# Two transformer layers behind a block of gathered experts: layers written out instead of looped, first norm applied after the projection, last down products in two halves

## The chip, the core and the metric

The kernel runs on one core of a Trainium2 chip. The metric is the time of one execution in microseconds (us) on the device; the runs of the kernel before have a median of 1599.08 us.

## What is computed

The reference is a transformer block with product-key experts, then two layers of a second kind, all for 256 rows of width 1024. What matters here is the end of the first block and the layers:

```python
# end of the first block
x = x + g2x * peer(hx2, ...)            # sum over 8 heads x 16 gathered experts for each row
x = rmsnorm(x, final_norm_g)            # final norm of the first block
# second block, two layers
for l in range(2):
    h = rmsnorm_2(x, norm1[l])
    p = h @ w_in[l]                     # columns: q 512, k 128, v 128, u 512
    q = rope(rmsnorm_2(q, q_norm[l])); k = rope(rmsnorm_2(k, k_norm[l]))
    y_f = fourier_mix(u, ...);  y_a = windowed_gqa(q, k, v, sink[l])
    x = x + concat(rmsnorm_2(y_f), rmsnorm_2(y_a)) @ w_o[l]
    h = rmsnorm_2(x, norm2[l])
    up = dwconv_centred(h @ w_up[l], ...)
    x = x + (silu(gate) * val) @ w_down[l]
return x
```

A norm is a scale per row (1 over the root of the row's mean square) and a gain per column. The scale of a row can be applied to the rows of a product instead of to its input.

## The kernel before

The 256 rows are two chunks of 128 partitions, `xr[:, c, :]`. A product in the layers is split in high and low parts: ScalarE rounds a piece of 128x1024 weights to fp32r (`weight_high`, L537), VectorE makes the difference (`weight_rest`, L552), and TensorE computes high x high, high x low and low x high (L1055 to L1057; L1219 to L1221 for the up product). A layer's pieces are 10 for the in-projection (0 to 3 q, 4 and 5 k and v, 6 to 9 u), 8 for the out-projection from `P_O` on, 44 for up from `P_UP`, 22 for down from `P_DOWN`. Three buffers for high and three for low parts go round. The weights come in slots of 2 MB through a ring of four slots, loaded by SyncE's queue in a fixed order; a slot is loaded when the low parts of the slot four before it are done.

The rows of a norm go through TensorE as eight tiles of 128 columns: the old program multiplies the rows with a diagonal that holds the scales (`split_tiles`, L1047), ScalarE takes out the high part with the gain (`tiles_high`, L559), VectorE the rest (`tiles_rest`, L565). So the tiles wait for the row statistics: squares of chunk 0 on ScalarE (L1248), of chunk 1 on VectorE (L1750), variance (L1544, L1545), a root on ScalarE (L1253) and four small steps (`newton`, L1550 to L1553).

Ahead of the layers, the last of 16 stages of gathered experts runs on chunk 1: VectorE makes a dot product of each of 16 gathered rows (L1822), groups of them get their weights (gelu on ScalarE L1389, `wts` on VectorE L1813), ScalarE makes a diagonal of each weight (L1393), and TensorE adds the expert's row (L984). `LAST_ENDS` says after which expert of the last stage weights are handed over. Then VectorE adds the sums to `xr` (`gated`, L1758 and L1759) and applies the block's final norm (L1864).

The order on each engine is that of the code; semaphores tie the engines. The layers are a loop `Fori(0, LAYERS)` on every engine, with the values that waits compare to computed in registers.

## Time and profile before

| what | value |
|---|---|
| runs | 1604.11, 1599.08, 1597.44 us, median 1599.08 |
| profiled execution | 1601.58 us, its span 1599.7 us |
| TensorE busy | 1381.5 us, 86% of the span |
| VectorE busy | 1085.2 us, 68% |
| ScalarE busy | 608.1 us, 38% |
| mean granted TensorE clock | 0.932 of full speed |

The span is the time from the first to the last instruction of the core. PE is TensorE's matmuls, PEld its weight loads, DVE VectorE, ACT ScalarE, POOL GpSimd, SP SyncE. The two layers lie from about 946 us to the end; the last stage of experts ends at 946 us, layer 0 ends at 1271 us, layer 1 at 1593 us.

### The profile page before, as it was taken

To read this page: it belongs to the slowest core of one execution; us is meant where nothing else is said; L and a number is where in the kernel's file an instruction comes from. 1 tells how busy PE (TensorE), PEld (TensorE's weight loads), DVE (VectorE), ACT (ScalarE), POOL (GpSimd) and SP (SyncE) were. 2 spreads that over 40 slices of the span, in tenths; PEclk is the share of its full clock that TensorE was granted. 3 is DMA by queue.
4 is the path that set the end of the run, shared out by engine and by line. 5 is a ranking of instruction groups with operands and counts; after the bars stand their busy time and mean duration, and the time that the engine had idled before them with its cause. 6 is when DMAs were issued, how large, how long until landed. Compare 5 with 4: busy or idle time off the path is not lost.

```text
span 1599.7 us, 19900 instructions
## 1 busy us (share of the span) xinstructions
PE 1381.5 (86%) x6272; PEld 960.2 (60%) x6272; DVE 1085.2 (68%) x2236; ACT 608.1 (38%) x1225; POOL 275.2 (17%) x263
## 2 busy tenths in 40 slices
PE   7998879778797979797987959979999799899998
PEld 2875675434343434343433427669998676699986
DVE  5598745666767676767677566657886466578863
ACT  5244641122222222222222124455665344456652
POOL 0000000633434444444444400000000000000000
PEclk9999979989898989898988989999999999999999
DMA  9425320999999999999999983144454431434440
GB/s 399 200 106 210 139 94 27 400 421 421 422 422 422 422 422 421 422 423 421 422 421 422 421 331 132 53 159 155 162 200 149 180 132 53 159 135 183 179 165 27
DMA packets 49266, 418.02 MB, mean 261 GB/s; under 512 B 5408, under 2 KB 5536, under 8 KB 6560
## 3 DMA queue, kind: packets, MB, share of 16 engines
q0 software_dynamic: 36864, 268.45, 40.4%
q1 hardware_dynamic: 12320, 148.51, 24.2%
q8 instruction: 47, 0.77, 0.2%
q14 instruction: 35, 0.29, 0.0%
HBM read 415.89 MB, written 1.05 MB: 261 GB/s over the span
## 4 chain that ended last, share of the span: by engine, by line
PE 50%; DMA 18%; DVE 12%; issue 10%; POOL 5%; ACT 3%; DVEq 0%; POOLq 0%; ACTq 0%; SPq 0%
DMA arena<-in_uv,ids 16%; PE ps L984 5%; PE ps L1219 5%; PE ps L1220 5%; PE ps L1221 5%; PE ps L1055 4%; PE ps L1057 4%; PE ps L1056 4%; POOL arena L718 3%; POOL ring L718 2%; PE ps L1105 2%; DMA ring<-in_b1w 2%; PE ps L1047 2%; PE ps L837 1%; DVE ring L1822 1%
## 5 line engine op out<-in xcount | busy, mean ns | idle before, releaser
L984 PE MATMUL ps<-ring,arena 128*128 128x512 f32 x512 | 256.5, 664 | 104.3 <-ACT arena L1393 104.3
L984 PEld LDWEIGHTS ps<-ring,arena 128*128 128x128 f32 x512 | 107.8, 214 | 248.4 <-issue 131.9
L1822 DVE CUSTOM_DVE_ANT_0 arena<-arena 128x1024 f32<-128x1024 f32 x128 | 157.0, 1227 | 132.4 <-DMA arena<-in_uv,ids 132.4
L718 POOL DMA_INDIRECT ring<-in_uv,ids x128 | 143.5, 1121 | 546.1 <-issue 306.6
L984 PE MATMUL ps<-arena 128*128 128x512 f32 x512 | 224.5, 596 | 6.8 <-ACT arena L1393 6.8
L552 DVE TENSOR_TENSOR arena_r<-ring,arena_r 128x1024 fp32r<-128x1024 f32 x152 | 185.2, 1224 | 66.3 <-ACT arena_r L537 66.3
L1219 PE MATMUL ps<-hH,arena_r 128*128 128x256 f32 x704 | 199.4, 283 | 0.0
L1220 PE MATMUL ps<-arena_r 128*128 128x256 f32 x704 | 199.2, 283 | 0.0
L1221 PE MATMUL ps<-hH,arena_r 128*128 128x256 f32 x704 | 199.2, 283 | 0.0
L537 ACT ACTIVATE arena_r<-ring 128x1024 fp32r<-128x1024 f32 x152 | 159.1, 1053 | 67.2 <-PE ps L1057 67.2
L984 PEld LDWEIGHTS ps<-arena 128*128 128x128 f32 x512 | 97.5, 191 | 131.6 <-issue 117.8
L1822 DVE CUSTOM_DVE_ANT_0 ring<-ring,arena 128x1024 f32<-128x1024 f32 x128 | 151.0, 1222 | 16.0 <-DMA ring<-in_uv,ids 15.5
L1393 ACT ACTIVATE arena<-cst,wts 128x128 f32<-128x128 f32 x256 | 90.4, 395 | 177.2 <-DVE wts L1813 90.0
L718 POOL DMA_INDIRECT arena<-in_uv,ids x128 | 131.1, 1024 | 86.9 <-PE ps L984 65.4
L1220 PEld LDWEIGHTS ps<-arena_r 128*128 128x128 f32 x704 | 135.2, 192 | 0.0
L1221 PEld LDWEIGHTS ps<-hH,arena_r 128*128 128x128 f32 x704 | 135.2, 192 | 0.0
L1219 PEld LDWEIGHTS ps<-hH,arena_r 128*128 128x128 f32 x704 | 135.2, 192 | 0.0
L1057 PE MATMUL ps<-arena_r 128*128 128x512 f32 (+1 forms) x336 | 127.4, 379 | 0.0
L1055 PE MATMUL ps<-arena_r 128*128 128x512 f32 x240 | 94.3, 393 | 2.6 <-DVE arena_r L583 2.1
L1056 PE MATMUL ps<-arena_r 128*128 128x512 f32 x240 | 93.4, 389 | 0.0
L1389 ACT ACTIVATE gel<-dots 128x4 f32<-128x4 f32 (+1 forms) x66 | 13.5, 205 | 195.5 <-DVE dots L1822 195.4
L1521 ACT ACTIVATE arena<-ps,lp 128x256 f32<-128x256 f32 x88 | 49.8, 566 | 96.5 <-DVE arena L1996 54.1
(272 smaller groups left out, 2105.2 us busy)
## 6 DMA issues: line engine op xcount, KB each, us to landing
ring<-in_lw SPq DMA_DIRECT2D x42, 2048.0 KB, 8.5
ring<-in_b1w SPq DMA_DIRECT2D x18, 2048.0 KB, 9.0
wqb<-in_wq SPq DMA_DIRECT2D x8, 1024.0 KB
ring<-in_lw SPq DMA_DIRECT2D x6, 1024.0 KB, 5.1
ring<-in_uv,ids POOLq DMA_INDIRECT x128, 22.3
arena<-in_uv,ids POOLq DMA_INDIRECT x128, 23.3
cst<-in_const SPq DMA_DIRECT2D x1, 1736.0 KB, 21.3
skb<-in_ctx SPq DMA_DIRECT2D x1, 1024.0 KB, 14.1
```

Of the source, the lines that this page charges most:

```text
L537: nc.scalar.activation(wH[p % PIECES], piece_raw(p), ACT.Copy).then_inc(w_hi, 1)
L552: nc.vector.tensor_tensor(wL[p % PIECES], piece_raw(p), wH[p % PIECES].bitcast(F32), ALU.subtract)\
L718: pool.indirect_dma_start(pairs_at[k], None, uv, bass.IndirectOffsetOnAxis(ap=ids[:, c, k:k + 1], axis=0))\
L984: last = nc.tensor.matmul(ps[:, 4 + 2 * c + b, :], diag[:, k % 4, :], vrows[k][:, b * 512:(b + 1) * 512], start=False, stop=(close and k = ...
L1055: nc.tensor.matmul(dst, ah, wH[p % PIECES][:, cols_], start=first, stop=False, skip_group_check=True)
L1056: nc.tensor.matmul(dst, ah, wL[p % PIECES][:, cols_], start=False, stop=False, skip_group_check=True)
L1057: last = nc.tensor.matmul(dst, al, wH[p % PIECES][:, cols_], start=False, stop=end, skip_group_check=True)
L1219: nc.tensor.matmul(dst, high, hH[:, k, :], start=(k == 0), stop=False)
L1220: nc.tensor.matmul(dst, high, hL[:, k, :], start=False, stop=False)
L1221: last = nc.tensor.matmul(dst, wL[p % PIECES][:, k * P:(k + 1) * P], hH[:, k, :], start=False, stop=(k == KD - 1))
L1393: nc.scalar.activation(diag[:, k % 4, :], ident, ACT.Copy, scale=wts[:, c, k:k + 1])\
L1822: V.tensor_tensor_reduce(out=urows[k], in0=urows[k], in1=hrow[:, c, :], scale=1.0, scalar=0.0, op0=ALU.mult, op1=ALU.add, accum_out=dots[: ...
```

## The change

It has five parts. The layers are written out (no loop; `lpv` reads the layer's parameters in place, so the copy `lp` goes). The first norm of a layer is no longer applied ahead of the projection: TensorE transposes the raw rows (`raw_tiles`, four tiles when the left half of `xr` is ready, four when the right half is), and the row scales `rs1` are applied when ScalarE takes the projection out. In layer 0 the final norm of the first block is taken out in the same way: its gain goes into the layer's gain (`fgc`), its scale `pre` into `rs1`. The high and low parts of pieces 0 and 1 get buffers of their own and are made ahead of the layer's opening. The last three down pieces compute their left halves first, then their right halves; `xr` is added up in halves, and the output is stored in four parts. The last stage of experts hands over at other places (`LAST_ENDS`).

```diff
-LAST_ENDS = (4, 8, 12, 14, 15, 16)
+LAST_ENDS = (4, 8, 10, 12, 13, 14, 15, 16)
...
+        first_wH = [area(kb, PIECE, of=arena_r) for kb in (0, 22)]
+        first_wL = [area(kb, PIECE, of=arena_r) for kb in (4, 8)]
...
+        def high_of(l, p):
+            return first_wH[p] if p < 2 else wH[(l * (PL - 2) + p - 2) % PIECES]
+
+        def low_of(l, p):
+            return first_wL[p] if p < 2 else wL[(l * (PL - 2) + p - 2) % PIECES]
+
+        def buffers_free(act, l, p):
+
+            if p >= 2 + PIECES:
+                act.wait_ge(piece_used, l * PL + p - PIECES + 1)
+            elif l == 0 and p < 2:
+                act.wait_ge(pair_free, NS + TOPK * (STAGES - 1) + 12)
+            elif l == 0:
+                act.wait_ge(l_half, 2)
+            elif p < 2:
+                act.wait_ge(piece_used, (l - 1) * PL + P_DOWN + 12)
+            else:
+                act.wait_ge(piece_used, l * PL + p - 2 - PIECES + 1)
...
-            with sp.Fori(0, LAYERS - 1) as l:
+            for l in range(LAYERS):
...
-            sp.wait_ge(l_x, LAYERS + 1)
-            sp.dma_start(out.rearrange("(c p) d -> p c d", p=P), xr[:, :, :]).then_inc(out_done, 16)
-            sp.wait_ge(out_done, 16)
+            for i in range(4):
+                c, part = i % 2, slice((i // 2) * 512, (i // 2 + 1) * 512)
+                sp.wait_ge(dn_out, 4 * LAYERS - 3 + i)
+                sp.dma_start(out[c * P:(c + 1) * P, part], xr[:, c, part]).then_inc(out_done, 16)
+            sp.wait_ge(out_done, 64)
...
+                def raw_tiles(*tiles):
+
+                    for k in tiles:
+                        if k >= 6:
+                            pe.wait_ge(lo_out, l * S_TILES + S_NORM1 + k - 5)
+                        for c in range(NC):
+                            last = nc.tensor.transpose(stile(S_NORM1, k)[:, c * P:(c + 1) * P], xr[:, c, k * P:(k + 1) * P],
+                                                       ident)
+                        last.then_inc(stile_done, 1)
...
-                pe.wait_ge(l_rows, 2 * l + 1)
-                split_tiles(S_NORM1, xr)
-
-                rows_by(0, 512, (4, 5), hH, hL, S_NORM1)
+                pe.wait_ge(l_half, 2 * l + 1)
+                raw_tiles(0, 1, 2, 3)
+                rows_by(0, 512, (4, 5), hH, hL, S_NORM1, (0,))
+                pe.wait_ge(l_half, 2 * l + 2)
+                raw_tiles(4, 5, 6, 7)
+                rows_by(0, 512, (4, 5), hH, hL, S_NORM1, (1, 2, 3))
...
+                for k in range(FT - PIECES):
+                    down(k, range(2))
+                for k in range(FT - PIECES, FT):
+                    last = down(k, (0,), False)
+                last.then_inc(dn_half, 1)
+                for k in range(FT - PIECES, FT):
+                    down(k, (1,))
...
-            table(ACT.Sqrt)
+            weight_high(act, 0, 0)
             act.wait_ge(wo_out, 6)
             squares(xr, ss, 0, 1, waste=junk_h)
             act.sem_inc(sq_done, 1)
-            roots(2, 5)
-
-            with act.Fori(0, LAYERS) as l:
+            weight_high(act, 0, 1)
+
+            act.wait_ge(l_par, 1)
+            for l in range(LAYERS):
                 off = l * (L_TILES // 2)
-                chain.enter(l, 9)
-                table(ACT.Sqrt)
-                act.wait_ge(l_x, l + 1)
-                squares(xr, ss, 0, 1)
-                act.sem_inc(sq_done, 1)
-                roots(2, l * 4 + 6)
-                weight_high(act, l, 0)
-                act.wait_ge(l_par, l + 1)
-                tiles_high(act, l, S_NORM1, hH, lpv("n1"))
-                weight_high(act, l, 1, 2, 3, 4)
+                tiles_high(act, l, S_NORM1, hH, lpv(l, "n1"))
+                weight_high(act, l, 2)
+                if l == 0:
+                    table(ACT.Sqrt)
+                    roots(2, 5)
+                    weight_high(act, l, 3)
+                    act.wait_ge(l_x, 1)
+                    squares(xr, ss, 0, 1)
+                    act.sem_inc(sq_done, 1)
+                    weight_high(act, l, 4)
+                    roots(2, l * 4 + 6)
+                else:
+                    squares(xr, ss, 0, 1)
+                    act.sem_inc(sq_done, 1)
+                    weight_high(act, l, 3)
+                    roots(2, l * 4 + 6)
+                    weight_high(act, l, 4)
+                act.wait_ge(l_scale, l + 1)
...
+                            nc.scalar.activation(qraw2[:, c, :], src, ACT.Copy, scale=rs1[:, c:c + 1]).then_inc(lproj_out, 1)
...
+                if l + 1 < LAYERS:
+                    weight_high(act, l + 1, 0, 1)
+                    table(ACT.Sqrt)
...
-            for c in range(NC):
-                dve.wait_ge(pair_free, NS + TOPK * (STAGES - 1 + c))
-                gated(g2b, [(c, n, 4 + 2 * c + n) for n in range(2)], 4 + 2 * c)
-            square_of_chunk1()
-            dve.wait_ge(sq_done, 5)
-            variance(2, D)
-            newton(2, 5)
-            for c in range(NC):
-                run(V.scalar_tensor_tensor(xr[:, c, :], xr[:, c, :], rstd[:, c:c + 1], con("fg"), ALU.mult, ALU.mult))
-            dve.wait_ge(lpar_in, 16)
+            dve.wait_ge(pair_free, NS + TOPK * (STAGES - 1))
+            gated(g2b, [(0, n, 4 + n) for n in range(2)], 4)
+            weight_rest(dve, 0, 0, 1)
+            dve.wait_ge(pair_free, NS + TOPK * STAGES)
+            for n in range(2):
+                gated(g2b, [(1, n, 6 + n)], 6 + n)
+                dve.sem_inc(l_half, 1)
...
+                def statistics(call, *between):
+
                     square_of_chunk1()
-                    if call == 6:
-                        V.tensor_copy(lp[:, :], lps[:, bass.ds(l, 1), :].rearrange("p a n -> p (a n)")).then_inc(l_par, 1)
-                    dve.wait_ge(sq_done, l * 4 + call)
+                    dve.wait_ge(sq_done, call)
                     variance(2, D)
-                    newton(2, l * 4 + call)
+                    weight_rest(dve, l, *between)
+                    newton(2, call)
+
+                tiles_rest(dve, l, S_NORM1, hL, hH, lpv(l, "n1"))
+                weight_rest(dve, l, 2)
+                if l == 0:
+                    statistics(5, 3)
+                    run(V.tensor_copy(pre, rstd[:, 0:2]))
+                    dve.wait_ge(stile_done, S_NORM1 + KD)
                     for c in range(NC):
-                        last = V.tensor_scalar(scale_diag[:, c, :], ident, rstd[:, c:c + 1], None, ALU.mult)
-                    last.then_inc(l_rows, 1)
-
-                normed(6)
-                dve.wait_ge(l_par, l + 1)
-                weight_rest(dve, l, 0)
-                tiles_rest(dve, l, S_NORM1, hL, hH, lpv("n1"))
-                weight_rest(dve, l, *range(1, P_O - 2))
+                        run(V.scalar_tensor_tensor(xr[:, c, :], xr[:, c, :], pre[:, c:c + 1], con("fg"), ALU.mult, ALU.mult))
+                    dve.sem_inc(l_x, 1)
+                    statistics(6, 4)
+                    run(V.tensor_tensor(rs1, rstd[:, 0:2], pre, ALU.mult))
+                else:
+                    statistics(l * 4 + 6, 3)
+                    run(V.tensor_copy(rs1, rstd[:, 0:2]))
+                    weight_rest(dve, l, 4)
+                dve.sem_inc(l_scale, 1)
+                weight_rest(dve, l, *range(5, P_O - 2))
...
-                dve.wait_ge(piece_used, (l + 1) * PL)
-                for i in range(4):
-                    dst = xr[:, i % 2, (i // 2) * 512:(i // 2 + 1) * 512]
-                    V.tensor_tensor(dst, dst, ps[:, 4 + i, :], ALU.add).then_inc(dn_out, 1)
-                dve.wait_ge(dn_out, 4 * l + 4)
-                dve.sem_inc(l_x, 1)
-                chain.leave(LAYERS)
+                if l + 1 < LAYERS:
+                    weight_rest(dve, l + 1, 0, 1)
+                for n in range(2):
+                    if n == 0:
+                        dve.wait_ge(dn_half, l + 1)
+                    else:
+                        dve.wait_ge(piece_used, (l + 1) * PL)
+                    for c in range(NC):
+                        dst = xr[:, c, n * 512:(n + 1) * 512]
+                        V.tensor_tensor(dst, dst, ps[:, 4 + 2 * n + c, :], ALU.add).then_inc(dn_out, 1)
+                    dve.wait_ge(dn_out, 4 * l + 2 * n + 2)
+                    dve.sem_inc(l_half, 1)
```

On TensorE nothing is added or taken in the products; the 16 matmuls of a first norm's tiles become 16 transposes. On VectorE 301 register instructions of the loop's body go.

The order of VectorE's instructions between the experts and layer 0. Before (`xr` the rows, `sm` small vectors, `arena` scratch; L1759 is the last addition of chunk 1, L1864 the final norm, the branch the loop's entry):

```order
L1759 TENSOR_TENSOR xr<-xr,arena 128x512
L1750 ISA arena,sm<-xr 128x1024
L1750 ISA sm 128x1
L1544 TENSOR_SCALAR sm<-sm 128x2
L1545 RECIPROCAL sm<-sm 128x2
L1550 TENSOR_TENSOR sm<-sm 128x2
L1551 TENSOR_TENSOR sm<-sm 128x2
L1552 TENSOR_SCALAR sm<-sm 128x2
L1553 TENSOR_TENSOR sm<-sm 128x2
L1864 SCALAR_TENSOR_TENSOR xr<-xr,sm,cst 128x1024 x2
L1871 UNCONDITIONAL_BRANCH
```

The same engine and place after the change (L573 is a low part of weights, L1811 and L1812 an addition of half a chunk, L589 the rests of the tiles):

```order
L1812 TENSOR_TENSOR xr<-xr,arena 128x512
L573 TENSOR_TENSOR arena_r<-ring,arena_r 128x1024 x2
L1811 TENSOR_TENSOR arena<-ps,wqb 128x512
L1812 TENSOR_TENSOR xr<-xr,arena 128x512
L1811 TENSOR_TENSOR arena<-ps,wqb 128x512
L1812 TENSOR_TENSOR xr<-xr,arena 128x512
L589 SCALAR_TENSOR_TENSOR arena_r<-ps,lps,hH 128x256 x8
L573 TENSOR_TENSOR arena_r<-ring,arena_r 128x1024
L1803 ISA arena,sm<-xr 128x1024
L1803 ISA sm 128x1
```

Two low parts of weights now stand between the additions of chunk 0 and those of chunk 1, and the statistics have moved behind the tiles' rests.

ScalarE at the same place, before (L1243 loads a table, L1248 squares of chunk 0, L537 a high part of weights, L559 high parts of tiles; L127, L1252 and L370 are waits):

```order
L1243 ACT_TABLE_LOAD
L1243 ACTIVATE sm<-cst 128x1
L127 ISA
L1428 REGISTER_ALU
L1248 ACTIVATE arena,sm<-xr 128x1024
L127 REGISTER_ALU
L1252 ISA
L1253 ACTIVATE sm<-sm 128x2
L370 ISA
L537 ACTIVATE arena_r<-ring 128x1024
```

And after, from the last diagonal on (L558 is the high part, L1289 the squares, L583 the tiles' high parts, L1294 the root, L1493 the eviction of q):

```order
L558 ACTIVATE arena_r<-ring 128x1024
L1289 ACTIVATE arena,sm<-xr 128x1024
L558 ACTIVATE arena_r<-ring 128x1024
L583 ACTIVATE hH<-ps,lps 128x256 x8
L558 ACTIVATE arena_r<-ring 128x1024
L1284 ACT_TABLE_LOAD
L1284 ACTIVATE sm<-cst 128x1
L1294 ACTIVATE sm<-sm 128x2
L558 ACTIVATE arena_r<-ring 128x1024
L1289 ACTIVATE arena,sm<-xr 128x1024
L558 ACTIVATE arena_r<-ring 128x1024
L1294 ACTIVATE sm<-sm 128x2
```

The first high part now stands ahead of the squares of chunk 0, and each further one between two steps of the statistics.

## Rows read from the trace of the kernel before

**Rows 1.** Windows: stretch, its us, PE, PEld, DVE, ACT, POOL busy, granted clock, DMA, GB/s

```profile
1084.00:1210.00 126.00, 126.00 (x1053) 126.00 (x1052) 105.71 (x170) 78.52 (x128) 0.00 (x0) 1.00 0.48 177
...
1210.00:1271.00 61.00, 60.81 (x272) 50.17 (x271) 28.82 (x30) 24.91 (x29) 0.00 (x0) 1.00 0.49 182
...
958.50:965.00 6.50, 6.46 (x33) 6.46 (x34) 3.97 (x7) 3.19 (x7) 0.00 (x0) 0.56 0.01 3
```

**Rows 2.** Timeline, last stage of experts: start, us, instruction, idle before it

```profile
920.63 7.13 PE L984 MATMUL ps<-ring,arena 128*128 128x512 f32 x16 [2.70 <-ACT arena L1393]
...
930.57 15.43 PE L984 MATMUL ps<-arena 128*128 128x512 f32 x32 [2.81 <-ACT arena L1393]
...
928.72 1.23 DVE L1822 CUSTOM_DVE_ANT_0 arena<-arena 128x1024 f32<-128x1024 f32 x1 [1.25 <-DMA arena<-in_uv,ids]
...
931.20 1.22 DVE L1822 CUSTOM_DVE_ANT_0 arena<-arena 128x1024 f32<-128x1024 f32 x1 [1.12 <-DMA arena<-in_uv,ids]
...
938.05 0.22 DVE L1813 SCALAR_TENSOR_TENSOR wts<-prob,pz,gel 128x1 f32<-128x1 f32 x1 [0.56 <-ACT gel L1389]
...
946.11 0.69 DVE L1758 TENSOR_TENSOR arena<-ps,wqb 128x512 f32<-128x512 f32 x1 [3.79 <-PE ps L984]
```

**Rows 3.** Timeline of TensorE: scaled tiles of layer 0, and piece 5

```profile
958.54 6.52 PE L1047 MATMUL ps<-arena,xr 128*128 128x128 f32 x32 [12.54 <-DVE arena L1883]
...
979.67 0.39 PE L1055 MATMUL ps<-arena_r,hH 128*128 128x256 f32 x1 [0.51 <-DVE arena_r L552]
```

**Rows 4.** SyncE, the first three weight loads of layer 0, and their times to landing

```profile
936.12 1.29 SPq L667 DMA_DIRECT2D ring<-in_lw  x3
...
DMA to landing us min/median/max: 8.1/10.2/14.6
```

**Rows 5.** Timeline, the steps of layer 0's opening on ScalarE and VectorE

```profile
942.41 1.06 ACT L1248 ACTIVATE arena<-xr 128x1024 f32<-128x1024 f32 x1 [1.26 <-DVE xr L1759]
...
964.57 1.52 DVE L565 SCALAR_TENSOR_TENSOR arena_r<-ps,lp,hH 128x256 fp32r<-128x256 f32 x3 [0.37 <-ACT hH L559]
...
976.33 1.09 ACT L1443 ACTIVATE arena<-ps 128x512 f32<-128x512 f32 x2 [4.38 <-PE ps L1057]
...
977.30 2.96 ACT L537 ACTIVATE arena_r<-ring 128x1024 fp32r<-128x1024 f32 x3
...
978.39 3.50 DVE L552 TENSOR_TENSOR arena_r<-ring,arena_r 128x1024 fp32r<-128x1024 f32 x3 [5.18 <-ACT arena_r L537]
```

**Rows 6.** Timeline of TensorE, four transposes in the scores of layer 0

```profile
1041.49 0.60 PE L1148 MATMUL ps<-cst,arena 128*128 128x128 f32 x4
```

**Rows 7.** Timeline of VectorE, small steps in straight code and in the loop

```profile
951.51 0.16 DVE L1553 TENSOR_TENSOR sm<-sm 128x2 f32<-128x2 f32 x1
...
951.71 2.61 DVE L1864 SCALAR_TENSOR_TENSOR xr<-xr,sm,cst 128x1024 f32<-128x1024 f32 x2
...
957.80 0.16 DVE L1553 TENSOR_TENSOR sm<-sm 128x2 f32<-128x2 f32 x1
...
958.00 0.48 DVE L1883 TENSOR_SCALAR arena<-cst,sm 128x128 f32<-128x128 f32 x2
```

**Rows 8.** Timeline between the layers, VectorE and ScalarE

```profile
1270.85 2.48 DVE L2027 TENSOR_TENSOR xr<-xr,ps 128x512 f32<-128x512 f32 x4 [5.84 <-PE ps L1057]
...
1276.54 1.22 DVE L1750 CUSTOM_DVE_ANT_0 arena<-xr 128x1024 f32<-128x1024 f32 x1 [3.21 <-issue]
...
1267.94 1.28 ACT L1243 ACT_TABLE_LOAD   x1 [4.19 <-issue]
...
1299.78 3.50 DVE L552 TENSOR_TENSOR arena_r<-ring,arena_r 128x1024 fp32r<-128x1024 f32 x3 [5.18 <-ACT arena_r L537]
```

**Rows 9.** Timeline of VectorE's last instructions, and DMA issues: size, us to landing

```profile
1592.85 2.48 DVE L2027 TENSOR_TENSOR xr<-xr,ps 128x512 f32<-128x512 f32 x4 [5.84 <-PE ps L1057]
...
out_x<-xr SPq DMA_DIRECT2D x1, 1024.0 KB, 3.9
...
cst<-in_const SPq DMA_DIRECT2D x1, 105.5 KB, 2.0
```

132 lines of the change are left out of this document (65 added, 67 removed).

## The prediction

> **What bounds the kernel now.** I read the stages by windows first, then the timeline of each place where one stage hands over to the next. Inside the two layers TensorE is the bound for most of the time: it is busy for the whole 126.0 us of the 44 up pieces and for 60.8 us of the 61 us of the 22 down pieces [rows 1]. That makes 126/44 = 2.86 us for a piece of 24 products of 256 columns and 60.8/22 = 2.76 us for a piece of 12 products of 512 columns. The change leaves the number of these products alone, so nothing is won there. What it touches are three hand-overs: from the last experts to layer 0, from layer 0 to layer 1, and from layer 1 to the output. I work out for each when "piece 5" of the in-projection starts, the last piece before the heads' norm chain, because everything behind it (squares, rotation, scores) is the same before and after and simply shifts with it.
>
> **The hand-over from the experts (before).** TensorE does experts 4 to 7 in 7.13 us, then waits, and does 8 to 15 from 930.57 in 15.43 us, to 946.0 [rows 2]. VectorE waits 3.79 us for that end and starts adding chunk 1 at 946.11. Then come square, statistics and final scaling of both chunks, a second square and second statistics, the diagonal, and only at 958.54 does TensorE start again, with scaled tiles that take 6.52 us [rows 2, 3]. Piece 5 starts at 979.67 [rows 3].
>
> **Single last experts.** After the change the last stage hands weights over after experts 4, 8, 10, 12, 13, 14, 15, 16. The dot products come every 2.48 us: the group that starts TensorE at 930.57 covers four of them, and with two the weights are ready two products, about 5 us, earlier, which is before TensorE has finished experts 4 to 7 at 927.8. From there it is fed: a single expert takes 7.13/4 = 1.8 us, 8 to 11 end at 934.9, and 12, 13, 14 follow close on their weights. The last weight is at 938.05 [rows 2], its diagonal some 0.7 us later, and the last expert ends at about 941.5, some 4.5 us earlier. Added are two more small weights on VectorE and two on ScalarE, at 0.22 us each, in time in which both wait for gathers.
>
> **Low parts first takes this gain back.** In the new order VectorE adds chunk 0, then makes the low parts of pieces 0 and 1, and only then adds chunk 1. These low parts wait for ScalarE's high parts, and these for the first 2 MB of layer weights. Its load is issued at 936.12, when the last gather has landed, and lands 8.1 us later, at 944.2 (the smallest of the three in the row) [rows 4]. From there: high part 0 (1.0 us each, 2.96 for three [rows 5]) to 945.3; low part 0 (3.50 for three, 1.23 with its latency) to 946.5; meanwhile ScalarE squares chunk 0 (1.06 and some 0.2 more) to 946.5, high part 1 to 947.55, low part 1 to 948.8. Chunk 1 is added from 948.8 on, **2.7 us later than before**, although the experts ended 4.5 us sooner. Queued behind that wait are all of chunk 1's additions, and behind them TensorE's tiles. The four operations take 2.9 us: the left half is done at 950.3, the right one at 951.7.
>
> **Raw tiles, scales later.** Now TensorE starts at 950.3 with transposes of unscaled rows. Four transposes of 128x128 take 0.60 us [rows 6] where the 16 scaled products took 6.52. But TensorE has stood since 941.5, and the clock will be at its lower level, 1.2 GHz, as it was in the stretch of the scaled tiles, where the row shows 0.56 [rows 1]. Those tiles used to take the slow time on themselves; now piece 0 does. Four tiles: 950.3 to 952. VectorE's rests, 0.51 us each (three in 1.52) [rows 5], start at 951.7, so tiles 0 and 1 are ready at 952.75. Piece 0 takes 2.76 us at the full clock and 5.4 at half; I take 4.0, since the clock came back some way into the scaled tiles: end at 956.7. The other four tiles follow: 956.7 to 957.9. ScalarE has their high parts at 958.95 (0.5 each, like VectorE's), then high part 2 to 960.0, VectorE low part 2 to 961.3, piece 2 on TensorE to 964.05. Then statistics stand between the low parts. Square of chunk 1 1.2 us and two small steps to 962.9, root 963.1, high part 3 to 964.2, low part 3 to 965.4, the four small steps 0.8, a copy 0.2, final scaling of both chunks 2.61 [rows 7]: 969.0. Second square 1.3 and variance to 971.0; ScalarE squares chunk 0 from 969.1, high part 4 to 971.4, low part 4 to 972.65, four small steps and a product: the projection's scale is ready at 973.65. ScalarE takes out q (two in 1.09) to 974.75, makes high part 5, VectorE low part 5, and **piece 5 starts at 977.1**. Before, the same tail after piece 3 is seen in [rows 5]: 976.33, 977.30, 978.39. Gain: 979.67 - 977.1 = **2.6 us**. With the full clock in piece 0 it is 3.8, with half the clock throughout 1.4.
>
> **Between the layers.** Call T the moment when the last down product ends: 1270.8. Before: adding 2.48 us, then VectorE stands 3.21 and ScalarE 4.19 with nothing that they wait for, at the loop's jump back; then square, the copy of the layer's parameters, statistics, diagonal, scaled tiles. Piece 5's low part starts at 1299.78 [rows 8], so piece 5 at about 1301.0 (1.28 behind it, as in layer 0: 978.39 and 979.67): **T + 30.2**. After: the last three pieces do their left halves first. The third one needs its low part 2.7 us after the fourth-last piece ends, and it is there at 2.4 (the splitting of a piece is ScalarE 1.06, VectorE 1.23 behind the freed buffer), so nothing stalls. The right halves take 3 x 1.38 = 4.1 us, in which VectorE makes the two low parts of layer 1 and adds the left half. At T TensorE turns four tiles at once; VectorE adds the right half (half of 2.48) to T + 1.3, makes two rests to T + 2.3. Piece 0 to 5.1, four tiles to 6.2, piece 1 to 8.9. High parts of tiles to 7.35, high part 2 to 8.4, low part 2 to 9.65, square 10.9, variance 11.3, low part 3 12.5, four steps and copy 13.5, low part 4 14.7. TensorE: piece 2 to 12.4, piece 3 to 15.3. From there the known tail of 3.35: evictions 1.09, high part 5, low part 5. **Piece 5 at T + 18.6.** Gain **11.6 us**. This is the large term, and it needs the clock to stay up: TensorE's holes are about 1.3 us here, where it used to stand for the whole hand-over.
>
> **The end.** Before, from the last product at 1592.8: 2.48 us of adding, one store of 1 MB that lands in 3.9 us, span end at 1599.7, so 6.9 us [rows 9]. After: the left half is added and on its way before the last product ends; behind it come 1.3 us of adding and two stores of 256 KB, the second issued at + 1.4. A store's time lies between 2.0 (the 105.5 KB load) and 3.9; I take 2.4, nearer to the small one: + 3.8, and 0.4 to the span's end. Gain **2.7 us**, between 1.2 and 3.1.
>
> **The layers written out.** The register instructions that computed wait values in the loop are gone, 301 of them on VectorE. Do they cost something? A chain of small steps advances 0.20 us a step in straight code (951.51 to 951.71) and 0.20 in the loop (957.80 to 958.00) [rows 7]. I take 0. The jump back is counted above. The Trainium skill (Runtime: NRT & Kernel Launch, "Instruction fetch mechanics") says that a taken branch outside the window stalls for its code while straight code is prefetched; the 3.21 and 4.19 us at the jump are in line with it. By that rule the written-out layers have no such stall, as in my sum.
>
> **Sum.** 2.6 + 11.6 + 2.7 = 16.9 us. The profiled execution's own time is 1601.58 (span 1599.7): it becomes 1584.7. The median of the runs is 1599.08, 2.5 lower, and what the comparison will go by: **1582.2 us**.
>
> **Rivals.**
> (a) The clock takes part of it back. The openings have holes of 1 to 2 us on TensorE, and between experts 7 and 8 a hole of 2.8 us was enough for the slow start that makes eight experts 15.43 instead of 14.26 [rows 2]. If piece 0 is slow throughout in layer 0 (+1.2) and pieces 0 and 1 of layer 1 are slow too (tiles 4 to 7 2.6 us later, piece 3 to 19.5, piece 5 at T + 22.8: +4.2), the gain is 11.5 and the time 1587.6. The Trainium skill (TensorE: Matmul & The Clock Gate, "Part 4: PE-mode transpose") states that transposes do not count as busy for the clock as matmuls do. By it the raw tiles, unlike the scaled ones, wake nothing, and this rival is what would happen; no stretch of this trace has transposes behind a low clock, so it is not tested here.
> (b) More than I count: the register instructions do cost where two engines answer each other (the scores of eight head groups, about 40 answers a layer). At 0.1 us an answer it is 8 us for both layers: 1574. The equal steps in [rows 7] speak against it.
> (c) No change within the measurement: the chain behind piece 5 is held by something else that doesn't shift. Against it: in the code nothing but ScalarE's evictions and squares stands between piece 5 and VectorE's norm of the heads. Its time: only 2.7 at the end and a few at the jump, 1592 to 1597.
> (d) Slower. Written out, the layers' code is twice as long, and all of it comes in by DMA beside the weights. If TensorE, which eats it fastest, ran dry, each time at the 3 to 4 us that the jump cost, it would take five such stalls to eat the 16.9 and eight to be slower by over 0.5%. Against it: the first pass through the loop is straight code too, and the 126 us stretch has no hole [rows 1].
>
> **Chances.** The sum as worked out, 0.70 (own range 1577 to 1586); (a) 0.14; (b) 0.08; (c) 0.05; (d) 0.03. A measurement of this kernel can tell about 0.5% from no change, 8 us: faster means under 1591.1. Faster takes the sum, (a) and (b) and a little of (c): 0.94; same 0.04; slower 0.02. The range for 8 in 10 takes (a) in and half of (b): **1575 to 1588**. The terms' own bounds make it no wider: +1.2/-1.2 at the first hand-over, +1.5/-0.4 at the end, and some 3 us between runs.
>
> **What the profile after would show.** Right: the last experts end near 941.5, and VectorE's additions of chunk 1 start near 948.8 behind a wait for ScalarE's high part 1; TensorE idle about 9 us there; piece 5 near 977; after the last down product of layer 0 piece 5 about 18.6 us later, with no VectorE idle time put down to issue; about 4.2 us from the last product to the end; up and down stretches at 126.8 and 60 us as before. Wrong: the granted clock at half in layer 1's opening, or TensorE holes between pieces 1 to 4 longer than 1 us, would say that the statistics between the low parts are too dear; more than 20 us gained would say that the loop's instructions cost something in the layer's body.

## The result, and the profile after

The changed kernel takes 1584.29 us (median of four runs, 1583.28 to 1588.16), against 1599.34 for four runs of the kernel before: a ratio of 0.9912, 95% interval 0.9894 to 0.9930, or 15.05 us less. That is more than the half per cent that can be told from no change, and 2.1 us above the 1582.2 that were forecast. Its profiled execution took 1588.16 us (span 1586.4), the slowest of the four, so the spans differ by 13.3 us only.

| what | before | after |
|---|---|---|
| span of the profiled execution | 1599.7 | 1586.4 |
| TensorE busy | 1381.5 (86%) | 1377.8 (87%) |
| VectorE busy | 1085.2 (68%) | 1082.2 (68%) |
| ScalarE busy | 608.1 (38%) | 606.1 (38%) |
| granted TensorE clock, mean | 0.932 | 0.938 |

**The last experts and the start of layer 0.** The timeline after; each row is start, us, instruction, and in brackets the idle time before it and what ended it. TensorE, VectorE and ScalarE in turn (L1005 experts, L1066 raw tiles, L1084 the first product of a group, L1875 dot product, L1811 and L1812 additions, L573 and L558 low and high parts of weights, L589 and L583 those of the tiles, L1803 square of chunk 1, L1952 the heads' norm). They answer to [rows 2, 3, 5].

```profile
928.45 14.11 PE L1005 MATMUL ps<-arena 128*128 128x512 f32 x32
950.92 1.94 PE L1066 MATMUL ps<-cst,xr 128*128 128x128 f32 x8 [8.37 <-DVEq L1917]
953.78 0.80 PE L1084 MATMUL ps<-arena_r,hH 128*128 128x512 f32 x1 [0.92 <-DVE arena_r L589]
...
958.28 1.03 PE L1066 MATMUL ps<-cst,xr 128*128 128x128 f32 x8
...
973.81 0.39 PE L1084 MATMUL ps<-arena_r,hH 128*128 128x256 f32 x1 [4.14 <-DVE arena_r L573]
...
978.27 0.34 PE L1084 MATMUL ps<-arena_r,hH 128*128 128x256 f32 x1
```

```profile
937.00 1.23 DVE L1875 CUSTOM_DVE_ANT_0 arena<-arena 128x1024 f32<-128x1024 f32 x1 [1.09 <-DMA arena<-in_uv,ids]
...
946.02 1.23 DVE L573 TENSOR_TENSOR arena_r<-ring,arena_r 128x1024 fp32r<-128x1024 f32 x1 [2.85 <-ACT arena_r L558]
948.17 1.23 DVE L573 TENSOR_TENSOR arena_r<-ring,arena_r 128x1024 fp32r<-128x1024 f32 x1 [0.92 <-ACT arena_r L558]
949.31 0.68 DVE L1811 TENSOR_TENSOR arena<-ps,wqb 128x512 f32<-128x512 f32 x1
...
951.60 0.69 DVE L1812 TENSOR_TENSOR xr<-xr,arena 128x512 f32<-128x512 f32 x1
...
959.20 1.66 DVE L589 SCALAR_TENSOR_TENSOR arena_r<-ps,lps,hH 128x256 fp32r<-128x256 f32 x4 [4.69 <-ACT hH L583]
...
962.39 1.22 DVE L1803 CUSTOM_DVE_ANT_0 arena<-xr 128x1024 f32<-128x1024 f32 x1
...
976.94 2.36 DVE L573 TENSOR_TENSOR arena_r<-ring,arena_r 128x1024 fp32r<-128x1024 f32 x2 [2.33 <-ACT arena_r L558]
...
983.98 1.22 DVE L1952 TENSOR_REDUCE sm<-arena 128x16 f32<-128x1024 f32 x1 [3.19 <-ACT arena L1503]
```

```profile
944.87 1.06 ACT L558 ACTIVATE arena_r<-ring 128x1024 fp32r<-128x1024 f32 x1 [5.29 <-DMA ring<-in_lw]
...
958.70 1.57 ACT L583 ACTIVATE hH<-ps,lps 128x256 fp32r<-128x256 f32 x4 [5.32 <-PE ps L1066]
```

The experts end at 942.56 (forecast 941.5; before 946.0), 4.3 us earlier after the last gathered row than before. The 32 matmuls start 3.0 us earlier, at 928.45, since the first group behind experts 4 to 7 is smaller, and they run 1.3 us shorter, without the slow start of [rows 2]. VectorE then stands 2.85 and 0.92 us behind ScalarE's high parts, and ScalarE 5.29 us behind the first weights. So chunk 1 is added only from 949.31 (forecast 948.8; before 946.11), and TensorE stands 8.37 us. All three waits stand where the prediction put them. The weights were issued at 936.99 here and at 936.12 before [rows 4]; the last gather landed 0.87 us later in this execution. I take that for chance: over the fourteen profiled executions of this document it landed anywhere from 933.7 to 938.9, with no order by kernel. Piece 5 starts at 978.27: 1.4 us earlier than before, 2.3 us with that 0.87 taken out. The forecast was 2.6. TensorE also stands 4.14 us ahead of piece 4, whose low part is queued behind the statistics, and piece 4 then takes 4.46 us (973.81 to 978.27) where it took 2.9 before.

**Between the layers**, VectorE and TensorE after, which answer to [rows 8] (L2095 additions, two operations to a row):

```profile
1268.01 1.28 DVE L2095 TENSOR_TENSOR xr<-xr,ps 128x512 f32<-128x512 f32 x2
1271.74 1.28 DVE L2095 TENSOR_TENSOR xr<-xr,ps 128x512 f32<-128x512 f32 x2 [2.46 <-PE ps L1086]
...
1289.41 3.49 DVE L573 TENSOR_TENSOR arena_r<-ring,arena_r 128x1024 fp32r<-128x1024 f32 x3 [3.44 <-ACT arena_r L558]
1296.44 1.22 DVE L1952 TENSOR_REDUCE sm<-arena 128x16 f32<-128x1024 f32 x1 [3.54 <-ACT arena L1503]
```

```profile
1271.54 1.03 PE L1066 MATMUL ps<-cst,xr 128*128 128x128 f32 x8
1274.11 0.50 PE L1084 MATMUL ps<-arena_r,hH 128*128 128x512 f32 x1 [1.53 <-DVE arena_r L589]
...
1276.98 1.04 PE L1066 MATMUL ps<-cst,xr 128*128 128x128 f32 x8
...
1281.32 0.47 PE L1084 MATMUL ps<-arena_r,hH 128*128 128x512 f32 x1 [0.57 <-DVE arena_r L573]
...
1290.69 0.39 PE L1084 MATMUL ps<-arena_r,hH 128*128 128x256 f32 x1 [0.76 <-DVE arena_r L573]
```

The last product ends at T = 1271.7. No idle time is put down to issue any more. The steps come at T + 2.4, 5.3, 9.6 and, for piece 5, 19.0; forecast were 2.3, 5.1, 9.65 and 18.6. Before it was T + 30.2.

**The end**, VectorE, which answer to [rows 9], and the page's line on the stores:

```profile
1582.62 1.28 DVE L2095 TENSOR_TENSOR xr<-xr,ps 128x512 f32<-128x512 f32 x2 [2.80 <-PE ps L1086]
```

```profile
out_x<-xr SPq DMA_DIRECT2D x4, 256.0 KB, 2.0
```

From the last product to the end of the span it is 3.8 us (forecast 4.2, before 6.9), with 2.0 us for a store of 256 KB where 2.4 were taken.

**The granted clock**, windows: stretch, its us, PE, PEld, DVE, ACT and POOL busy, granted clock, DMA share, GB/s. They answer to [rows 1].

```profile
947.00:957.50 10.50, 5.66 (x17) 4.52 (x18) 5.81 (x10) 2.75 (x5) 0.00 (x0) 0.51 0.84 357
974.00:978.00 4.00, 4.00 (x22) 4.00 (x22) 1.56 (x5) 3.15 (x4) 0.00 (x0) 0.57 0.00 0
1035.50:1043.00 7.50, 6.53 (x8) 2.71 (x9) 1.05 (x5) 0.29 (x3) 0.00 (x0) 0.54 0.00 0
1085.00:1211.00 126.00, 126.00 (x1053) 126.00 (x1052) 105.88 (x171) 78.34 (x128) 0.00 (x0) 1.00 0.48 177
...
1262.00:1290.00 28.00, 25.84 (x131) 21.19 (x129) 16.82 (x29) 14.62 (x23) 0.00 (x0) 1.00 0.47 180
```

The up stretch is what it was: busy throughout, at full clock. Between the layers the clock stays at 1.00 through raw tiles and holes. At the experts' end it goes to its lower level, 1.2 GHz, after TensorE has stood from 942.56 to 947.0, and stays there over the raw tiles and the larger part of piece 0. It falls a second time at 974.4, behind the 4.14 us that TensorE stands and 0.6 us into piece 4, and stays low over that piece until 977.8. This stretch is new too: before, the clock was at 1.00 there. The row at 1035.5 is new as well: before, that place of layer 0 ran at full clock. It is TensorE's products of 512 columns for the Fourier mix, first before, then after:

```profile
1037.54 3.67 PE L1036 MATMUL ps<-ring,arena 128*128 128x512 f32 x8 [1.97 <-DVE arena L1922]
```

```profile
1036.47 6.75 PE L1057 MATMUL ps<-ring,arena 128*128 128x512 f32 x8 [1.81 <-DVE arena L1981]
```

Eight matmuls take 6.75 us instead of 3.67.

### The profile page after: what moved, and what is told of

Same layout as the page of the kernel before. It is cut to its first block, busy times and chain, and to the rows that moved or that the text cites. A ratio compares the mean times of both kernels' runs of the same rounds, so it can differ in the third digit from the quotient of the medians.

```text
span 1586.4 us, 18714 instructions
## 1 busy us (share of the span) xinstructions
PE 1377.8 (87%) x6240; PEld 952.9 (60%) x6240; DVE 1082.2 (68%) x2236; ACT 606.1 (38%) x1225; POOL 272.8 (17%) x263
## 3 DMA queue, kind: packets, MB, share of 16 engines
q1 hardware_dynamic: 12624, 148.52, 24.7%
## 4 chain that ended last, share of the span: by engine, by line
PE 49%; DMA 17%; DVE 14%; issue 9%; POOL 6%; ACT 4%; POOLq 0%; DVEq 0%; ACTq 0%; SPq 0%
DMA arena<-in_uv,ids 15%; PE ps L1252 5%; PE ps L1254 5%; PE ps L1253 5%; PE ps L1005 5%; PE ps L1084 4%; PE ps L1085 4%; PE ps L1086 4%; POOL arena L739 3%; POOL ring L739 2%; PE ps L1138 2%; DVE ring L1875 2%; DMA ring<-in_b1w 2%; PE ps L858 2%; PE ps L859 1%
## 5 line engine op out<-in xcount | busy, mean ns | idle before, releaser
L1005 PE MATMUL ps<-ring,arena 128*128 128x512 f32 x512 | 255.8, 663 | 106.0 <-ACT arena L1434 106.0
L1005 PEld LDWEIGHTS ps<-ring,arena 128*128 128x128 f32 x512 | 107.5, 213 | 250.0 <-issue 131.5
L1875 DVE CUSTOM_DVE_ANT_0 arena<-arena 128x1024 f32<-128x1024 f32 x128 | 156.9, 1226 | 134.6 <-DMA arena<-in_uv,ids 124.6
L573 DVE TENSOR_TENSOR arena_r<-ring,arena_r 128x1024 fp32r<-128x1024 f32 x152 | 185.2, 1223 | 63.9 <-ACT arena_r L558 63.9
L1005 PE MATMUL ps<-arena 128*128 128x512 f32 x512 | 224.2, 594 | 3.7 <-ACT arena L1434 3.7
L1252 PE MATMUL ps<-hH,arena_r 128*128 128x256 f32 x704 | 199.4, 283 | 0.0
L558 ACT ACTIVATE arena_r<-ring 128x1024 fp32r<-128x1024 f32 x152 | 159.1, 1053 | 68.7 <-PE ps L1086 63.0
L1005 PEld LDWEIGHTS ps<-arena 128*128 128x128 f32 x512 | 96.5, 190 | 129.2 <-issue 116.2
L1875 DVE CUSTOM_DVE_ANT_0 ring<-ring,arena 128x1024 f32<-128x1024 f32 x128 | 151.0, 1221 | 16.0 <-DMA ring<-in_uv,ids 15.5
L1252 PEld LDWEIGHTS ps<-hH,arena_r 128*128 128x128 f32 x704 | 135.1, 192 | 0.0
L1084 PE MATMUL ps<-arena_r 128*128 128x512 f32 x240 | 94.4, 393 | 1.9 <-DVE arena_r L607 1.6
L1430 ACT ACTIVATE gel<-dots 128x4 f32<-128x4 f32 (+2 forms) x68 | 13.9, 204 | 205.4 <-DVE dots L1875 205.3
L1572 ACT ACTIVATE arena<-ps,lps 128x256 f32<-128x256 f32 x88 | 49.6, 564 | 96.8 <-DVE arena L2058 57.3
```

Source lines behind the costliest of these rows:

```text
L558: nc.scalar.activation(high_of(l, p), piece_raw(p), ACT.Copy).then_inc(w_hi, 1)
L573: nc.vector.tensor_tensor(low_of(l, p), piece_raw(p), high_of(l, p).bitcast(F32), ALU.subtract)\
L1005: last = nc.tensor.matmul(ps[:, 4 + 2 * c + b, :], diag[:, k % 4, :], vrows[k][:, b * 512:(b + 1) * 512], start=False, stop=(close and k = ...
L1084: nc.tensor.matmul(dst, ah, high_of(l, p)[:, cols_], start=first, stop=False, skip_group_check=True)
L1252: nc.tensor.matmul(dst, high, hH[:, k, :], start=(k == 0), stop=False)
L1875: V.tensor_tensor_reduce(out=urows[k], in0=urows[k], in1=hrow[:, c, :], scale=1.0, scalar=0.0, op0=ALU.mult, op1=ALU.add, accum_out=dots[: ...
```

## The experiments

Twelve kernels were run, each in four to twelve executions beside the kernel before on the same chip. The median of before was 1600.27 beside the first four, 1599.76 beside the next four, 1601.41 beside the three after them and 1599.44 beside the last; so the ratios are compared, or the medians within a group. For each profiled execution I take the distances between five marks. g is the start of the last gathered row's dot product; the layer's first weights are issued in the same moment, so differences in the gathers fall out. c1 is the end of chunk 1's additions, sq the start of its square on VectorE, hn the start of the heads' norm (the first operation that is the same in all), T the start of VectorE's additions behind the last down product. The row of after is worked out from the rows above (937.00, 951.60 + 0.69, 962.39, 983.98, 1271.74, 1296.44); the others from the same places of their traces. The distances of a row are those of one execution. Where a low stretch of the clock lies over TensorE's work, a distance grows by 0.8 to 3 us without any edit: the scaled tiles of layer 0, the same code, take 6.76 us in e1 and 5.31 in e2.

| kernel | median us | ratio to before (95%) | g to c1 | g to sq | g to hn | hn to T | T to hn, layer 1 | hn to T, layer 1 | T to end |
|---|---|---|---|---|---|---|---|---|---|
| before | 1599.34 | | 12.9 | 12.9 | 48.9 | 285.8 | 35.6 | 286.4 | 6.9 |
| changed | 1584.29 | 0.9912 (0.9894 to 0.9930) | 15.3 | 25.4 | 47.0 | 287.8 | 24.7 | 286.2 | 3.8 |
| e1 | 1594.66 | 0.9970 (0.9958 to 0.9982) | 13.1 | 13.2 | 49.4 | 284.0 | 31.8 | 285.7 | 6.9 |
| e2 | 1591.68 | 0.9944 (0.9927 to 0.9960) | 13.1 | 13.2 | 47.9 | 285.8 | 31.2 | 286.0 | 3.8 |
| e3 | 1585.09 | 0.9904 (0.9888 to 0.9921) | 15.1 | 25.8 | 48.3 | 285.7 | 24.7 | 285.8 | 3.7 |
| e4 | 1582.04 | 0.9884 (0.9866 to 0.9902) | 9.2 | 22.9 | 45.2 | 285.6 | 24.7 | 285.8 | 3.8 |
| e5 | 1585.47 | 0.9907 (0.9891 to 0.9924) | 13.1 | 25.8 | 47.9 | 285.5 | 24.7 | 285.8 | 3.8 |
| e6 | 1585.94 | 0.9909 (0.9888 to 0.9930) | 15.3 | 26.4 | 48.8 | 285.7 | 24.7 | 285.8 | 3.8 |
| e6t | 1584.58 | 0.9909 (0.9890 to 0.9928) | 15.5 | 25.4 | 47.8 | 285.7 | 24.7 | 285.8 | 3.8 |
| e7 | 1572.11 | 0.9838 (0.9818 to 0.9857) | 9.2 | 15.9 | 37.5 | 285.4 | 23.1 | 284.0 | 3.8 |
| e9 | 1572.13 | 0.9820 (0.9805 to 0.9835) | 9.2 | 16.6 | 38.2 | 285.4 | 23.1 | 284.0 | 3.8 |
| e10 | 1580.84 | 0.9883 (0.9863 to 0.9903) | 9.2 | 20.0 | 41.6 | 287.7 | 24.7 | 286.2 | 3.8 |
| e8 | 1571.60 | 0.9820 (0.9802 to 0.9838) | 9.2 | 15.9 | 37.5 | 285.7 | 23.1 | 284.1 | 3.8 |
| e11 | 1577.36 | 0.9868 (0.9845 to 0.9890) | 15.2 | 20.1 | 41.8 | 285.6 | 23.1 | 284.1 | 3.7 |

**e1, written out only.** The kernel before with the layers written out and nothing else.

```diff
-            with dve.Fori(0, LAYERS) as l:
+            for l in range(LAYERS):
```

> The kernel before with its two layers written out and nothing else. My sum: only the stall at the jump back goes, 3.1 us (VectorE's 3.21 us of idle time put down to issue between the layers); the steps inside the layers keep their 0.20 us, so the time is 1596. Rival (the register instructions cost something wherever engines answer each other): 8 us or more, 1591 or less. Rival (code comes in too slowly): slower than before.

Measured 1594.66, 4.8 us less by the ratio (2.9 to 6.7). The opening of layer 1, start of the rows on VectorE:

```profile
1267.39 2.48 DVE L2024 TENSOR_TENSOR xr<-xr,ps 128x512 f32<-128x512 f32 x4 [5.84 <-PE ps L1057]
1270.07 1.22 DVE L1748 CUSTOM_DVE_ANT_0 arena<-xr 128x1024 f32<-128x1024 f32 x1 [0.20 <-DVE xr L2024]
```

Between the additions and the square there are now 0.20 us where before there were 3.21 put down to issue. T to hn is 3.8 us shorter. The other distances also shrink: hn to T by 1.8 in layer 0 and 0.7 in layer 1. Of these, 0.6 to 0.7 us in each layer lies between hn and the second norm (91.85 to 91.18, 93.49 to 92.87), where the scores' small steps are and the wait values were computed. The other 1.1 us in layer 0 are the clock's. They lie in the scaled tiles of the second norm, first before, then e1:

```profile
1077.44 6.79 PE L1047 MATMUL ps<-arena,xr 128*128 128x128 f32 x32 [5.82 <-DVE arena L1883]
```

```profile
1075.12 5.58 PE L1047 MATMUL ps<-arena,xr 128*128 128x128 f32 x32 [5.72 <-DVE arena L1880]
```

Before, the granted clock fell at 1076.8, late in TensorE's idle time, and stayed low until 1083.7, over nearly all the tiles; in e1 it fell at 1072.0 and was back at 1078.8.

**e2, written out and halves.** Adds the last three down pieces in halves and the store in four parts.

```diff
+                for k in range(FT - PIECES, FT):
+                    last = down(k, (0,), False)
+                last.then_inc(dn_half, 1)
+                for k in range(FT - PIECES, FT):
+                    down(k, (1,))
```

> The same with the last three down pieces in halves, the left half added while the right one is computed, and the output stored in four parts; the norm still ahead of the projection. My sum: 2.7 to 3.1 us at the end (6.85 us from the last product to the span's end become 3.8), and 1.25 us between the layers (half of the 2.48 us of adding), so 4.2 us on top of the written-out kernel: 1592. What is left to the changed kernel's 1584.3, some 7.5 us, is then the price of the norm ahead of the projection. Rival: the halves are hidden or cost as much as they bring, same as written out only.

Measured 1591.68, 3 us below e1. The end is 3.1 us shorter, as in the changed kernel; between the layers only 0.6 us are won by it, not the 1.25 of half the additions.

**e3, old ends.** The changed kernel with the experts in the old groups.

```diff
-LAST_ENDS = (4, 8, 10, 12, 13, 14, 15, 16)
+LAST_ENDS = (4, 8, 12, 14, 15, 16)
```

> The changed kernel with the old places at which the last experts' weights are handed over (4, 8, 12, 14, 15, 16). My theory: the last expert ends 4.5 us later, near 947, but VectorE gets to chunk 1 only at 949.3, behind the low parts, so the single experts bring nothing: within 0.3 us of the changed kernel, 1584.3. Rival: they carry their full 4.5 us, then this is 1588.8.

Measured 1585.09, ratio 0.9904 against 0.9912. Its experts, and the start of chunk 1's additions on VectorE (g is 938.68):

```profile
933.12 15.70 PE L1005 MATMUL ps<-arena 128*128 128x512 f32 x32 [2.81 <-ACT arena L1434]
```

```profile
950.75 0.68 DVE L1811 TENSOR_TENSOR arena<-ps,wqb 128x512 f32<-128x512 f32 x1
```

The experts end 10.1 us after g instead of 5.6, yet chunk 1's additions start at g + 12.1, as with the new ends (+ 12.3). The single experts bring nothing in this order, as the prediction had it. That hn comes 1.3 us later after g than in the changed kernel is mostly the clock: piece 0 takes 5.3 us for 4.5 and piece 4 0.8 us more.

**e4, chunk 1 first.** The changed kernel with chunk 1's additions ahead of the two low parts on VectorE.

```diff
-            weight_rest(dve, 0, 0, 1)
             dve.wait_ge(pair_free, NS + TOPK * STAGES)
             for n in range(2):
                 gated(g2b, [(1, n, 6 + n)], 6 + n)
                 dve.sem_inc(l_half, 1)
+            weight_rest(dve, 0, 0, 1)
```

> The changed kernel, but VectorE adds chunk 1 (and releases the halves of xr) before the low parts of pieces 0 and 1. My theory: the low parts in front hold chunk 1 from 942.5 to 949.3. Without them the additions are done at 945.5, TensorE's tiles are there early, low part 1 ends at about 949.3 as now and two rests later, near 950.4, piece 0 starts (953.8 now): 3.4 us of gain at most, less what ScalarE's order (high parts and squares ahead of the tiles) takes: 1581.5. Rival: the low parts in front are right, and this only moves the same work: 1584.3.

Measured 1582.04, 3 us below e3 on the same chip; their intervals overlap, so the marks have to carry it (g to hn 45.2 against 48.3). Chunk 1 is done at g + 9.2 and TensorE has raw tiles early, but the first piece starts only 3.5 us earlier, since both parts of weight 1 now stand ahead of the tiles' parts. TensorE:

```profile
946.00 1.12 PE L1066 MATMUL ps<-cst,xr 128*128 128x128 f32 x8 [2.28 <-DVEq L1916]
951.47 0.79 PE L1084 MATMUL ps<-arena_r,hH 128*128 128x512 f32 x1 [4.35 <-DVE arena_r L589]
```

**e5, chunk 1 first, old ends**: the two edits above together.

> The changed kernel with two edits: the additions of chunk 1 of the residual stand ahead of the low part of weight 1 on VectorE's queue, and the last experts are taken in pairs again as before the change. Theory (single experts gain only when nothing else holds VectorE after the experts): the experts end 10.1 us after the last gather has landed instead of 5.6, chunk 1 is added at +13.1 instead of +9.2, and the first piece of layer 0 starts 3 to 4 us later than with single experts, so about 1585.3 us, like the changed kernel. Rival (the hand-over is set by something else, such as ScalarE's order or the clock of TensorE): the same as with chunk 1 first alone, 1582.

Measured 1585.47 (ratio 0.9907) against 1582.04 (0.9884) for e4. The intervals overlap; by the marks c1 comes 3.9 us and hn 2.7 us later. So the single experts are worth about 3 us, but only where VectorE takes chunk 1 first. With the old ends VectorE waits for TensorE there again:

```profile
946.32 0.69 DVE L1811 TENSOR_TENSOR arena<-ps,wqb 128x512 f32<-128x512 f32 x1 [3.81 <-PE ps L1005]
```

**e6 and e6t, fillers.** TensorE is kept at work where it stood 8.4 us, with products of zeros or with transposes.

```diff
+                if l == 0:
+                    for _ in range(8):       # e6t: 62 transposes of 128x128
+                        nc.tensor.matmul(ps[:, 0, :], zero, cst[:, 0:512], start=True, stop=True)
                 pe.wait_ge(l_half, 2 * l + 1)
                 raw_tiles(0, 1, 2, 3)
```

> The changed kernel with 8 products of zeros against 512 columns of float32 into a free bank of PSUM, issued on TensorE between the last expert and the raw tiles of layer 0, where it stands idle. The output is not touched. Theory (the granted clock costs time at the hand-over): the granted clock stays at 1.00 where it fell to 0.50 from 947 to 957.5 us, the first piece takes 2.8 us as the fourth does at full clock instead of 4.5, and about 2 us are gained: 1582.3. Rival (the first piece's time is set by the parts of the weights and the tiles that VectorE and ScalarE hand over): no gain, 1584.3, or slower by what the products run over the start of the raw tiles.

> The changed kernel with 62 transposes of a 128x128 float32 tile in the same place, which keep TensorE occupied for about as long as the 8 products of the other run. The output is not touched. Theory (whatever occupies TensorE holds its clock): the same as with the products, 1582.3. Rival: the granted clock falls at about 947 us as without them, and the time is that of the changed kernel, 1584.3. The Trainium skill (TensorE: Matmul & The Clock Gate, Part 4: PE-mode transpose) says that transposes do not count as activity for the clock; by that page this run goes by the rival.

Measured 1585.94 and 1584.58: no gain from either. First e6, then e6t, windows and TensorE's timeline (L1105 the fillers):

```profile
947.00:953.00 6.00, 3.76 (x15) 1.74 (x13) 4.38 (x6) 2.65 (x7) 0.00 (x0) 1.00 0.99 423
```

```profile
942.64 7.03 PE L1105 MATMUL ps<-cst,wk 128*128 128x512 f32 x16
951.07 1.09 PE L1066 MATMUL ps<-cst,xr 128*128 128x128 f32 x8 [1.40 <-DVEq L1920]
954.00 0.80 PE L1084 MATMUL ps<-arena_r,hH 128*128 128x512 f32 x1 [1.84 <-DVE arena_r L589]
...
959.29 0.92 PE L1066 MATMUL ps<-cst,xr 128*128 128x128 f32 x4
```

```profile
947.00:953.00 6.00, 2.64 (x23) 2.16 (x20) 4.69 (x7) 2.08 (x5) 0.00 (x0) 1.00 1.00 429
```

```profile
941.61 6.93 PE L1105 MATMUL ps<-cst 128*128 128x128 f32 x62
950.21 1.09 PE L1066 MATMUL ps<-cst,xr 128*128 128x128 f32 x8 [1.66 <-DVEq L1920]
953.15 0.50 PE L1084 MATMUL ps<-arena_r,hH 128*128 128x512 f32 x1 [1.85 <-DVE arena_r L589]
...
957.26 1.38 PE L1066 MATMUL ps<-cst,xr 128*128 128x128 f32 x8
```

Both hold the clock at 1.00 up to 953, where the changed kernel stood at 0.51. But in e6 it falls at 953.0, just before piece 0, which then takes 5.3 us (954.00 to 959.29) instead of 4.5; in e6t it falls at 954.5, and piece 0 takes 4.1. The tiles end earlier, but piece 0 starts no earlier after g (16.8 and 16.9 us, 16.8 in the changed kernel): the low stretch was shortened, and what is left of it lies on piece 0. TensorE had two holes of 1.4 to 1.9 us behind the fillers in both. The second low stretch, over piece 4, is longer here than in the changed kernel: in e6t the clock is at its lower level from 971.6 to 978.4 and piece 4 takes 5.3 us (4.5), which makes hn 0.8 us later. e3 to e5, without fillers, have that long second stretch as well. On the transposes the rival lost: the clock did not fall at 947. The Trainium skill's sentence that transposes do not count as busy (TensorE: Matmul & The Clock Gate, Part 4: PE-mode transpose) is not borne out here: 62 float32 transposes held the clock as eight products did. That is holding a clock that was already at 1.00; whether transposes alone would bring a low clock back, no run shows.

**e7, hand-over reordered.** Chunk 1 first as in e4, and besides: the squares of chunk 0 ahead of high part 0 on ScalarE, the parts of weight 1 between the tiles' halves, and on TensorE all eight raw tiles ahead of the first piece, in both layers.

```diff
                 pe.wait_ge(l_half, 2 * l + 1)
                 raw_tiles(0, 1, 2, 3)
-                rows_by(0, 512, (4, 5), hH, hL, S_NORM1, (0,))
                 pe.wait_ge(l_half, 2 * l + 2)
                 raw_tiles(4, 5, 6, 7)
-                rows_by(0, 512, (4, 5), hH, hL, S_NORM1, (1, 2, 3))
+                rows_by(0, 512, (4, 5), hH, hL, S_NORM1)
...
-                tiles_rest(dve, l, S_NORM1, hL, hH, lpv(l, "n1"))
+                tiles_rest(dve, l, S_NORM1, hL, hH, lpv(l, "n1"), (0, 1, 2, 3))
+                if l == 0:
+                    weight_rest(dve, l, 1)
+                tiles_rest(dve, l, S_NORM1, hL, hH, lpv(l, "n1"), (4, 5, 6, 7))
```

> The changed kernel with a further order of the hand-over: chunk 1 of the residual is added ahead of both low parts, the squares of chunk 0 stand ahead of the high part of weight 0 on ScalarE, the parts of weight 1 stand between tiles 0 to 3 and 4 to 7, and in both layers TensorE makes all eight raw tiles before the first piece. Theory (with chunk 1 added at +9.2, ScalarE's queue and the second wait for tiles hold the first piece): 1.9 us less in layer 0 than with chunk 1 first alone, and 0.9 us less in each layer from a first piece that does not stop, so about 1579. Rival (the first pieces are bound by the parts of weights 2 and 3, which come later in this order): 1582 or above.

Measured 1572.11, 7 us below the theory. Against e4, g to hn is 7.7 us shorter where 2.8 were expected, and T to hn and hn to T in layer 1 together 3.4 where 0.9 were. Which of the edits does it, the next two runs tell.

**e9 and e10, the two halves of e7.** e9 is e4 with TensorE's part of the diff above alone. e10 is e7 without it: the orders of VectorE and ScalarE alone.

> Chunk 1 first (1582.0 before), and on TensorE alone all eight raw tiles ahead of the first piece, in both layers; the orders of VectorE and ScalarE stay those of that run. It tells which half of the hand-over's new order brought 1572.1. Theory (the raw tiles of the second half between pieces 0 and 1 hold everything that VectorE and ScalarE do behind them: in the run with chunk 1 first both engines waited 5.7 and 6.5 us for them, and the low part of weight 2 came only then): most of the gain is here, pieces 1 to 3 follow piece 0 without a stop, between the layers the 24.7 us from the last additions to the heads' norm become 23.1, and the time is about 1574. Rival (the gain is in the order of the two other engines): 1580 or more.

> The other half: the orders of VectorE and ScalarE of the run with 1572.1, with raw tiles 4 to 7 on TensorE between pieces 0 and 1 as in the changed kernel. Theory (as in the other run): piece 0 starts 1.7 us earlier after the last gather than with chunk 1 first, but pieces 2 and 3 still wait for parts that stand behind tiles 4 to 7, so at best 1.7 us are gained on 1582.0: about 1580.3. Rival: 1574 or less.

Measured 1572.13 for e9 and 1580.84 for e10. One wait and one call moved on TensorE bring 10 us on e4: 7.0 in layer 0's opening, 1.6 between the layers, and 1.8 in layer 1's body, where a dip of the clock is missing (below). The order of the other two engines brings nothing that can be told, with it (e7 to e9) or without it (e10 to e4): in e10 g to hn is 3.6 us shorter than in e4 (0.7 of it by the clock over piece 4), and hn to T in layer 0 2.1 us longer again, which is the clock over the wide products. VectorE in e9 (g is 934.17), which is to be read beside VectorE's rows of the changed kernel above:

```profile
946.48 3.22 DVE L589 SCALAR_TENSOR_TENSOR arena_r<-ps,lps,hH 128x256 fp32r<-128x256 f32 x8
...
950.76 1.22 DVE L1802 CUSTOM_DVE_ANT_0 arena<-xr 128x1024 f32<-128x1024 f32 x1
...
972.38 1.22 DVE L1951 TENSOR_REDUCE sm<-arena 128x16 f32<-128x1024 f32 x1 [3.53 <-ACT arena L1502]
```

There VectorE stood 4.69 us behind ScalarE's parts of tiles 4 to 7, ScalarE 5.32 us behind TensorE's transposes of them, and these stood behind piece 0. Here all eight rests run in one row, and the square of chunk 1 starts at g + 16.6 instead of g + 25.4 (22.9 in e4, with chunk 1 first alone). From that square to hn it is 21.6 us in both (950.76 to 972.38, 962.39 to 983.98), and in all kernels of the new form it is either 21.6 or 21.7, or 22.2 to 22.5: the longer ones are e3 to e6t, in which piece 4 runs at the lower clock throughout. So what sets piece 5 is VectorE's way to that square, with the clock over piece 4 worth up to 0.8 us, and not when TensorE's pieces 0 to 3 are done.

**e8, reordered and filler.** e7 with three products of zeros.

> The order of the run with 1572.1, and 3 products of zeros against 512 float32 columns on TensorE between the last expert and the raw tiles of layer 0, into a free bank; the output is not touched. In that run the granted clock was 0.50 from 944 to 948 us, over the raw tiles, which took 3.4 us of 16 where 1.03 per 8 is their time at full clock. Theory (the raw tiles are now on the path, so their clock counts): about 1.3 us less, 1570.8. Rival (the lower clock only comes later, as it did with the fillers in the changed kernel): 1572.1 or a little more.

Measured 1571.60, ratio 0.9820 against 0.9838: no difference that can be told. From 942 to 950 the clock is 1.00 where e7 has 0.79, yet hn comes at g + 37.5 in both. The first piece starts at g + 11.6 in both: ScalarE has waited 0.59 us for the first weights to land, and the parts made from them are later than the tiles. First e7, then e8:

```profile
942.00:950.00 8.00, 5.31 (x25) 4.41 (x25) 7.59 (x12) 7.00 (x13) 0.00 (x0) 0.79 1.02 435
```

```profile
942.00:950.00 8.00, 6.62 (x25) 3.30 (x23) 7.45 (x12) 4.28 (x8) 0.00 (x0) 1.00 1.00 428
```

```profile
946.87 1.06 ACT L558 ACTIVATE arena_r<-ring 128x1024 fp32r<-128x1024 f32 x1 [0.59 <-DMA ring<-in_lw]
```

**e11, tiles first on the changed kernel.** TensorE's part of e7's diff on the changed kernel as it is.

> The changed kernel with one wait and one call moved on TensorE: all eight raw tiles ahead of the first piece, in both layers. The low parts of weights 0 and 1 still stand ahead of chunk 1's additions, as in the change. Theory (TensorE's order of the second half of the tiles alone holds pieces 2 and 3 and all that follows): chunk 1 is added at +15.3 as in the changed kernel, but the heads' norm of layer 0 starts some 7 us earlier after the last gather than its +46.98, between the layers 1.6 us and in the body of layer 1 another 1.7 us go, as they did with chunk 1 first: 1584.3 - 10.3, so about 1574. Rival (the gain needed chunk 1 first as well, since the first piece is then covered by its additions): 1580 or more.

Measured 1577.36 (ratio 0.9868). Some 7 us come from the order of the tiles without chunk 1 first; g to hn is 5.2 us shorter rather than 7, and the two places in layer 1 are worth what was expected. It fell between theory and rival. By the times it can't be told whether the two edits help each other (7 us here and 10 on e4, each to within some 4); by the marks the square comes 5.3 us earlier here and 6.3 from e4 to e9, so they do by about 1 us. TensorE's tiles start at g + 13.9 here and at g + 7.8 in e9, the square of chunk 1 at g + 20.1 and g + 16.6.

## Why the prediction was right, point by point

The forecast of 1582.2 with a range of 1575 to 1588 held; the changed kernel is at 1584.3. Measured by piece 5, as the sum was made, and the profiled executions (1599.7 and 1586.4):

| term | forecast | measured | by |
|---|---|---|---|
| experts to layer 0 | 2.6 | 2.3 | piece 5, with the later gather taken out |
| between the layers | 11.6 | 11.2 | T + 30.2 less T + 19.0 |
| from piece 5 to hn, both layers | 0 | -0.7 | 5.4 us before, 5.7 and 5.8 after |
| the end | 2.7 | 3.1 | 6.9 less 3.8 |
| bodies of the layers, hn to T | 0 | -1.8 in this execution | -2.0 and +0.2 in the table |

The measured column makes 14.1; less the 0.87 by which the gather came later, that is the 13.3 between the spans. The 0.7 that was lost from piece 5 to hn is in good part ScalarE's: it now applies the scale as it takes k and v out, four times 0.37 us instead of 0.28 in each layer, a term that the sum did not have. In e3 to e6t the bodies come out at +0.7 to +1.0 in sum, so the -1.8 is for the most part the clock in this one execution; what the changed kernel's other executions had is not on record.

**Low parts first takes the gain of the experts back: right**, and shown by e3 to e5, by their marks. The single experts end 4.6 us earlier and change nothing, until chunk 1's additions are moved ahead of the low parts; then they are worth 3.

**Raw tiles: right in time, wrong in what they showed me.** The steps came within 0.3 us of those worked out once the later gather is taken out, except piece 0 (4.5 us for 4.0). The bounds were a little off: half the clock throughout would have left 2.6 - 1.4 = 1.2, not 1.4, and 5.3 us was the most that piece 0 took. One of my signs of being wrong did come: a hole longer than 1 us between pieces 1 and 4, of 4.14 us ahead of piece 4 in layer 0 (in layer 1 the longest was 0.57). The sum's own times imply it, piece 3 at an end by 968.2 and low part 4 at 972.65, but it had no price for the clock that fell behind it. That this cost nothing was luck: piece 4 ended at 978.27, when low part 5 had just been made (976.94 + 1.23). In e3 to e6t the same stretch cost 0.8 us.

I also wrote the chain "piece 0, then four tiles, then their parts, then square, statistics" down as given and didn't ask what it would cost to let the tiles go first. It was worth 7 to 10 us, some 2 of them the missing dip of the clock in layer 1: TensorE put a piece of 2.8 to 5.3 us, which nobody waited for, ahead of 1 us of transposes for which two engines stood.

**Between the layers: right.** e1 says that 3.8 of the 10.9 us from T to hn are the jump, e2 that the halves bring 0.6, and the step from e2 to the changed kernel (31.2 to 24.7) that 6.4 are the raw tiles, the later scales and the parts made ahead.

**The jump.** Straight code has no such stall, by e1. e1 takes away the jump and the register work at the loop's edge together, so which of the two VectorE stood for is not separated. The Trainium skill (Runtime: NRT & Kernel Launch, "Instruction fetch mechanics") says that a taken branch stalls for its code; the trace is in line with it, with 0.20 us for 3.21.

**The register instructions: the term was sized 0 and is about 1.3 us.** Rival (b) put 8 us on them. e1 shows 0.62 and 0.67 us between hn and the second norm of each layer; that it is these instructions and not the clock is argued from the place, since no run took them away alone. The steps of one chain, on which I relied, don't show it. If it lies where the engines answer each other, about 40 times a layer, it is 0.016 us an answer, far below the 0.1 of the rival.

**Rival (a), the clock takes part back: half right, at another place.** Between the layers the clock stayed at 1.00. In the opening of layer 0 piece 0 took 4.5 us, and 5.3 in e3, e4 and e6, where the low stretch lay over all of it: that is the 1.2 us of the rival. The stretch over piece 4 is the same rival at a place where I had not looked. Nor had I counted the dip near 1036 us, which costs 1.5 to 3.1 us where it falls on the wide products. It takes back what the written-out layers give and more: hn to T in layer 0 is 284.0 in e1, which has no dip there, 285.4 to 285.8 in most of the others, which have a short one, and 287.8 after. The 285.8 of the kernel before are made otherwise: no dip there, but the slow tiles of the second norm and the register instructions. In layer 1 the same eight products take 5.37 us before and after and 3.67 in e9; e7, e8 and e11 lack that dip too, and in these four hn to T is 1.8 us shorter than in e3 to e6t. Whether the dip comes at all, and in which layer, changed with the order of the work far ahead of it. Why it comes where it does stays open; no run here moved it at will.

**Rivals (c) and (d)** are out: everything behind piece 5 shifted with it (the up pieces take 126.8 us as before), and neither the span behind it nor the code of the second layer shows a stall. Nor did the written-out layers bring more code by DMA: the page's two instruction queues moved 0.77 and 0.29 MB before, 0.70 and 0.20 MB after.

## What to carry to other kernels

When an engine's order has a short step that others wait for (transposes, an addition) and a long one that nobody waits for yet, put the short one first, even if the long one could start; look for the engine that stands in two rows of brackets, one behind the other, and ask what the first releaser was doing. An earlier end of one stage is worth nothing until the first instruction behind it on the waiting engine is the one that uses it: try both edits together before either is dropped. Keeping TensorE at work through one hole does not by itself make the work behind it fast: here it shortened one low stretch, left the next, and changed no time. Before two orders are compared by one trace each, see where the low stretches lie in both.

The version that came out best is e9, the changed kernel with chunk 1 first and all raw tiles first: 1572.1 us, ratio 0.9820 to the kernel before and below the changed kernel by 12 us in the medians and 15 by the ratios (they ran beside different executions of the kernel before). e7 and e8 can't be told from it.

## What the runs showed of the hardware that was not expected

- Transposes held the granted clock at 1.00 as products did (e6t): 6.93 us of them, then a hole of 1.66 us and the raw tiles, with no fall until 954.5.
- The clock fell under work as well as behind a long hole: in e6t at 954.5, 1.3 us into piece 0, behind holes of 1.66 and 1.85 us; in the changed kernel at 1035.5, in one of 1.81 us ahead of the wide products, and stayed there under them.
- A store of 256 KB landed in 2.0 us, where one of 1 MB took 3.9 [rows 9]. With the left half added early, that made the end 3.1 us shorter (e2); the two were not tried apart.
- At the loop's jump back VectorE stood 3.2 us with nothing to wait for [rows 8]; e1, without loop and register work, has 0.20 us there.
- The clock went to its lower level behind the same hole of some 4.1 us ahead of piece 4 for 3.4 us (changed kernel) or 6.8 us (e3 to e6t): 0.8 us of time on one piece, by what came before.
